# A two-block network on one core: the last projection tiles reordered, and the attention's first maxima and some convolution taps moved across a stage boundary

## What is computed

```python
# first block, chunks of 64 tokens, 4 heads
q, k, v, g_lr, r = split(h @ w_in)                     # 16 columns of g_lr
log_a = log_sigmoid(g_lr @ w_alpha + b_alpha) / 16     # then S_t = diag(a_t) S_{t-1} + k_t^T v_t
o = rmsnorm(q_t S_t per head) * silu(r);  x = rmsnorm(x + gate * (o @ w_out))
# second block
u = rms_norm(x) * (1 + scale) + shift;  p = u @ w_in
q, k = rope_2d(rms_norm(p_q)), rope_2d(rms_norm(p_k))  # 8 query heads, 2 key heads of 64
attn = softmax(q @ [k_ctx, k]^T / 8) @ [v_ctx, v] * silu(p_za)
y = depthwise_conv31(p_a * sigmoid(p_g)) + conv_b      # 512 channels, "124 taps" of 128 channels
conv = (silu(layer_norm(y)) @ w_pw + b_pw) * silu(p_zc)
out = x + gate * ([attn, conv] @ w_out)
```

## Time and profile before

| what | us |
|---|---|
| median of 3 executions (2685.8 to 2707.22) | 2698.7 |
| the profiled execution, its own time | 2696.7 |
| its span in the trace | 2694.9 |
| GLA, of the span | 65.2 to 1053.8 |
| projections, to the end of the last tile | 1063.8 to 1596.1 |
| from there to the attention's first score | 1596.1 to 1646.7 |
| attention's 32 steps | 1646.7 to 2431.7 |
| output | 2431.7 to 2694.9 |

### The profile page before, as it was taken

How to read it: one execution, slowest core, us unless ns; L and a number is a source line. 1 busy time by engine, 2 the same in 40 slices (tenths; PEclk the granted TensorE clock), 3 DMA queues, 4 the chain that set the end, 5 groups by cost and what they waited for, 6 DMA issues and landing times. The chain is left out here.

```text
span 2694.9 us, 34569 instructions
## 1 busy us (share of the span) xinstructions
PE 2495.9 (93%) x11297; PEld 1715.9 (64%) x11297; DVE 1716.4 (64%) x2698; ACT 1011.4 (38%) x1766; POOL 765.3 (28%) x353
## 2 busy tenths in 40 slices
PE   4898899999999998999999966999999999988998
PEld 1576677777777776777777753545544555546776
DVE  3236564654546351888997985777777777775664
ACT  4144453434344430322222124544454444542222
POOL 0233311101111110112202024666667666640000
PEclk8899999999999999999999986999999999998999
DMA  7964787378567747488767544111112101104334
GB/s 263 348 205 145 264 283 273 135 248 317 190 231 267 263 153 263 173 289 307 233 220 252 200 167 103 28 29 29 29 53 59 26 25 29 29 24 162 129 133 155
DMA packets 225098, 453.40 MB, mean 168 GB/s; under 512 B 23941, under 2 KB 82555, under 8 KB 224724
## 3 DMA queue, kind: packets, MB, share of 16 engines
q1 hardware_dynamic: 193928, 351.01, 38.6%
q10 hardware_dynamic: 31052, 100.87, 10.8%
HBM read 328.82 MB, written 109.35 MB: 163 GB/s over the span
## 5 line engine op out<-in xcount | busy, mean ns | idle before, releaser
L2098 DVE TENSOR_REDUCE att_mx<-att_bank_m 128x1 f32<-128x512 f32 (+1 forms) x640 | 365.3, 630 | 126.5 <-PE att_bank_m L1907 126.5
L2047 ACT ACTIVATE att_p_f<-att_bank_s 128x512 f32<-128x512 f32 x576 | 316.9, 597 | 304.4 <-PE att_bank_s L1948 293.5
L557 PE MATMUL gla_bank_g<-mid_a_hi,mid_w_hi 128*128 128x512 f32 x1024 | 417.2, 407 | 13.4 <-DVE mid_a_lo L1075 10.4
L557 PE MATMUL gla_bank_g<-mid_a_lo,mid_w_hi 128*128 128x512 f32 x1024 | 403.2, 394 | 0.0
L557 PE MATMUL gla_bank_g<-mid_a_hi,mid_w_lo 128*128 128x512 f32 x1024 | 403.2, 394 | 0.0
L1888 POOL TENSOR_TENSOR att_den<-att_den,att_p_f 128x1024 f32<-128x1024 f32 x160 | 379.6, 2373 | 59.6 <-ACT att_p_f L2047 48.7
L1611 DVE SCALAR_TENSOR_TENSOR proj_conv_acc<-proj_conv_in,proj_conv_w,proj_conv_acc 128x512 f32<-128x512 f32 (+1 forms) x480 | 362.0, 822 | 0.0
L1922 PE MATMUL att_bank_o<-att_p_f,att_v 128*64 128x512 f32 x1152 | 269.1, 602 | 0.0
L557 PEld LDWEIGHTS gla_bank_g<-mid_a_hi,mid_w_hi 128*128 128x128 f32 x1024 | 195.3, 191 | 77.6 <-issue 19.0
L557 PEld LDWEIGHTS gla_bank_g<-mid_a_hi,mid_w_lo 128*128 128x128 f32 x1024 | 194.7, 190 | 42.4
L557 PEld LDWEIGHTS gla_bank_g<-mid_a_lo,mid_w_hi 128*128 128x128 f32 x1024 | 195.4, 191 | 40.6 <-issue 2.7
(11 more groups left out here) (400 smaller groups left out, 4505.5 us busy)
## 6 DMA issues: line engine op xcount, KB each, us to landing
mid_w_hi<-scratch_w_hi SPq DMA_DIRECT2D x100, 512.0 KB, 4.5
mid_w_lo<-scratch_w_lo SPq DMA_DIRECT2D x100, 512.0 KB, 6.0
mid_w_hi<-scratch_w_hi ACTq DMA_DIRECT2D x84, 512.0 KB, 3.8
mid_w_lo<-scratch_w_lo ACTq DMA_DIRECT2D x84, 512.0 KB, 5.1
scratch_w_hi<-mid_w_hi SPq DMA_DIRECT2D x54, 512.0 KB, 6.2
scratch_w_lo<-mid_w_lo SPq DMA_DIRECT2D x54, 512.0 KB, 7.0
mod_wslab<-in_ada_w SPq DMA_DIRECT2D x6, 2048.0 KB, 17.9
first_w_raw<-in_gla_w_in SPq DMA_DIRECT2D x24, 512.0 KB, 6.5
```

The source lines that it names most:

```text
L557: last = pe.matmul(banks[s % 2][:], w[:, k, :], a[:, k, :], start=(k == 0 and n == 0), stop=(k == KT - 1 and n == 2))
L2047: act.activation(p_f[:, kt, :], S[kt % SBANKS][:], ACT.Exp, scale=float(HD) ** -0.5).then_inc(p_done, 1)
L2098: dve.reduce_max(mx[:, qt, n:n + 1], M[p % MBANKS][:, 0:min(TB, KEYS - TB * n)], AX_X).then_inc(mx_read, 1)
```

## The change

1. The two phases become one. The attention's functions are called inside the projections' program and get their semaphores and PSUM banks (S is BQ, BS, G0; M is BN, BX, BY, BV; the output bank is G1). No barrier stands between the two.
2. In the last block the tiles go in the order 0 to 3, 8 to 13 (q, k, v), 4 to 7, 14 to 21, and the chain of q and k runs 4 turns earlier (`chain_turn`). In every block k's head goes ahead of q's four. SP loads the keys and v of the first three blocks and the context at turn 2 of the last block, and its last 512 keys, q of the first two steps and the last v at turn 16 (7 DMAs, in front of the swap of the fifth head). ACT rounds them at turns 6 and 16.
3. The first step's 20 pieces stand on PE between the last gate tiles: 4 behind each of tiles 17 to 21. DVE takes the maxima of each 4 at the end of the following turn (18 to 21), behind that turn's gate and taps, and the last 4 after turn 21.
4. The last block's table has 86 of the 124 taps. The other 38 go to steps 0 to 6, 5 or 6 a step: 2 at kt 7, 2 at kt 10, the rest behind the column at kt 14.
5. The two multiplications and the addition of the rope are all on DVE (before, POOL had two of the three): 40 more instructions of 128x512 on DVE in the stage, 40 fewer on POOL.
6. In step 0, ACT rounds group 1's keys at kt 8 and sets its row of ones at kt 12; POOL makes their rest (5.05 us before). The first group's steps 1 to 7 are written out instead of looped.
7. GLA: the gate's weights are 32 columns (hi and lo side by side), so 16 matmuls instead of 24 a block; y's hi and lo have tensors of their own, so the next block's input can be rounded while the last w_out tiles run; the gating of six chunks of y takes their first 3/4 early and the last 128 tokens in 2 instructions over three chunks; ACT rounds 7 chunks of y ahead of the tanh of the last r tile; the sum of squares is made one tile earlier (between tiles 4 and 5 of w_out) and the split of the next input within tiles 5 and 6. The first u loads of the projections are issued by SP in the last block's turn 24 instead of after its last tile.
8. Output: other places in memory only.

```diff
     OWN = [[7] * 7 + [6] * 3 + [5] * 2 + [4, 3, 3, 4, 4, 5]] * 2 + [[7] + [6] * 8 + [7] + [6] * 2 + [5] * 2 + [4] * 4] + [
-        [8, 8, 8, 7, 8, 7, 8, 7, 8, 7] + [7, 7, 6, 6, 6, 6, 5, 5]]
+        [7] * 8 + [6] + [0] + [4, 4, 4, 3, 2, 2, 2, 3]]
+    HEADS = (4, 0, 1, 2, 3)
+    EARLY_TILES = 4
+    ORDER = [list(range(NW))] * (NB - 1) + [[0, 1, 2, 3] + list(range(8, 14)) + [4, 5, 6, 7] + list(range(14, NW))]
+    def chain_turn(b, j):
+        return j + EARLY_TILES if b == NB - 1 else j
...
+    SINGLE = 8
+    TAP_STEPS = 7
...
+                        if b == NB - 1 and j == 2:
...
+                            load_made()
+                        if b == NB - 1 and jq == 20:
+                            sp.wait_ge(v_stored, UP + 16 * NB)
+                            sp.wait_ge(q_stored, UP + 16 * (5 * (NB - 1) + 1))
+                            load_last()
...
+        def first_maxima(first):
+            if first == 0:
+                pe.wait_ge(k_hi_done, UP + 2)
+            for p in range(first, first + 4):
+                piece(0, 0, 0, p)
...
+                        if b == NB - 1:
+                            if j == 16:
+                                split_first_q()
+                            if j >= 18:
+                                first_maxima(4 * (j - 18))
+                first_maxima(16)
+                first_column()
+                rest()
...
+        def taps_of_step(dve, i, part):
+            if isinstance(i, int) and i < TAP_STEPS:
+                m0, m1 = last_tap[i], last_tap[i + 1]
+                third = -(-(m1 - m0) // 3)
+                keep["last_taps"](dve, min(m0 + third * part, m1), min(m0 + third * (part + 1), m1))
```

More of the change, by code:

```diff
@@ L551, in gemm @@
                     for k in range(KT):
-                        if k == BETWEEN_AT and between is not None:
+                        if k == between_at and between is not None:
                             between()
@@ new lines, in attention, with col, tiles_in @@
+    w_raw = [k_raw[0][:, D * n:D * (n + 1)] for n in range(2)]
+    y = k_raw[0][:, 0:NC * TB].rearrange("p (k n) -> p k n", k=NC)
+    acc, rs = (k_raw[1][:, TB * n:TB * (n + 1)] for n in (2, 3))
+    squares = (q_raw[0], q_raw[1])
+    tanhs = (den[0][:, 0, :], den[0][:, 1, :], q_raw[0][:], q_raw[1][:])
+    BM, BV = M[1], M[2]
+    def col(name, j):
+        at = VROWS[name][0] + j
+        return cols[:, at:at + 1]
+    def tiles_in(i):
+        return W_AT[i] if isinstance(i, int) and i in W_AT else ()
@@ new lines, in at_step, with need, pair, steps @@
+    def at_step(i, n):
+        return isinstance(i, int) and i == n
+    def need(eng, semaphore, n):
+        if isinstance(n, int) and n <= 0:
+            return
+        eng.wait_ge(semaphore, UP + n)
+    def pair(j):
+        return p_f[:, 2 * j:2 * j + 2, :]
+    def steps(eng, body):
+        last = GROUP_STEPS - 1
+        for g in range(NKV):
+            base = g * GROUP_STEPS
+            body(base, 0, g, g - 1 if g else None, g)
+            single = 2 if g else SINGLE
+            for n in range(1, single):
+                body(base + n, n % 2, g, g, g)
+            with eng.Fori(single // 2, GROUP_STEPS // 2 - 1) as it:
+                for s in range(2):
+                    body(it * 2 + (base + s), s, g, g, g)
+            body(base + last - 1, 0, g, g, g)
+            body(base + last, 1, g, g, g + 1 if g + 1 < NKV else None)
@@ new lines, in gpsimd, with rest_of_k, body @@
+    def gpsimd(pool):
+        def rest_of_k(n):
+            g, keys = K_PARTS[n]
+            pool.wait_ge(k_hi_done, UP + n + 1)
+            pool.tensor_tensor(k_b[g][0:HD, keys], k_raw[g][0:HD, keys], k_a[g][0:HD, keys].bitcast(F32), ALU.subtract).then_inc(k_lo_done, 1)
+        pool.wait_ge(k_hi_done, UP + 1)
+        pool.memset(mz[:], 0.0).then_inc(cleared, 1)
+        rest_of_k(0)
+        rest_of_k(1)
+        def body(i, s, g, before, after):
+            need(pool, den_sum, i - 1)
+            for j in range(1, POOL_ADDS + 1):
+                if j == 5 and at_step(i, 0):
+                    rest_of_k(2)
+                pool.wait_ge(p_done, UP + i * NKT + 2 * j + 2)
+                if j > 1:
+                    pool.wait_ge(den_pool, UP + i * POOL_ADDS + j - 1)
+                pool.tensor_tensor(den[s][:], pair(0) if j == 1 else den[s][:], pair(j), ALU.add).then_inc(den_pool, 1)
+            for n in tiles_in(i):
+                if n >= 2:
+                    pool.wait_ge(w_hi_done, UP + n + 1)
+                    pool.tensor_tensor(wo_lo[:, n - 2, :], w_raw[n % 2], wo_hi[:, n - 2, :].bitcast(F32), ALU.subtract).then_inc(w_lo_done, 1)
+        steps(pool, body)
@@ new lines, in body, with first_maxima, rest @@
+                            rest_wp(n)
+                    add_den(i, s, NPR - 2)
+                if kt == 17 and at_step(i, STEPS - 2):
+                    centre_y()
+        def first_maxima(first):
+            for p in range(first, first + 4):
+                reduce(0, p)
+        def rest():
+            steps(dve, body)
+            add_den(STEPS - 1, 1, NPR - 1)
+            fold_den(STEPS - 1, 1)
+            swish_y(0)
+            swish_y(1)
+            add_o(STEPS - 1)
+            swish_y(2)
+            invert(STEPS - 1)
+            swish_y(3)
+            finish(STEPS - 1)
+            for k in range(NC):
+                rest_y(k)
```

1252 lines of the change are left out of this document (652 added, 600 removed).

## The result

Four executions of the changed kernel took 2719.87 to 2736.26 us, median 2729.16; four of the kernel before 2685.8 to 2707.22, median 2699.74. The ratio is 1.0124 (95% interval 1.0094 to 1.0154): slower by 29 us, or 1.2%. The forecast was 2716 in a range of 2664 to 2745. The time lies in the range, but the largest chance, 0.47, stood on "within 1%", and slower by more had 0.31.

The account below looks back on a forecast made before the run. PE, with work in 93% of the span, was taken to bound the kernel, its clock second. 2696.7 - 18 - 3.5 + 0 - 6 + 45 = 2714.2, with 2.0 for the median 2716 us; range 2664 to 2745.

Parts of the forecast that it names:

- GLA's gain: GLA, part 7: fewer matmuls, shorter waits and less half clock, against a longer wait L658; -18 us, bounds -5 to -40.
- the step from a profiled execution to the median: Whole kernel: the median lies 2.0 us above the profiled execution, as before, making 2714.2 into 2716.
- The attention: Attention, parts 4 and 6: taps delay maxima and column, so PE waits and its clock falls; +45 us, bounds +5 to +60.
- One tap per addition: Attention: DVE gets in one tap per POOL addition, so two taps count as 4.2 us, not 1.4.
- The boundary: Between projections and attention, parts 1 to 3: overlap against waits behind tiles and half clock; -6 us, bounds -14 to +15.
- C: Rival: PE stays at half clock through the last gate tiles (10 us each) and most of steps 1 to 6; 2746 us, chance 0.16.
- The gap to the projections: GLA to projections: loads issued 7 tiles earlier shorten PE's 10.0 us wait; -3.5 us, between 0 and -4.5.
- the rope: Projections, blocks 0 to 2: ten more DVE operations a block, offset by fewer collisions with POOL; 0, between -3 and +6 us.
- the output: Output stage: nothing of its work changes; 0, within 2 us.
- the waits for y: GLA: of PE's 10.4 us of waits for the rests of y, 4 go.
- L658's wait: GLA block ends: PE's 5.7 us wait on DVE's chain stays and grows by 2 at each of three boundaries, 6 us.
- a second tap right behind the first: Attention: by the port lock it could keep the ports and cost 0.7 us, making the sum some 30 us less.

Follow-up runs that it names:

- e13: The changed kernel measured once more, with no edit, beside the other runs on one chip; median 2724.94 us, ratio 1.0107 to the kernel before.
- e1: The changed kernel without the 38 taps of the attention's steps 0 to 6; median 2680.29 us, ratio 0.9947 to the kernel before.
- e2: The changed kernel with all taps, POOL's additions in steps 0 to 6 left out but for 8 columns; median 2682.56 us, ratio 0.9946.
- e4: The changed kernel with DVE's four maxima of turns 18 to 21 at the head of the turn; median 2699.06 us, ratio 1.0018.
- e11: e7 with ACT's tanh of the last r tile in GLA behind 3 roundings of y instead of 7; 2680.58 us, ratio 0.9941.
- e12: e7 with e11's earlier tanh, the first q loaded early and block 0's w_out weights rounded ahead of the next input; 2677.55 us, ratio 0.9932.
- e15: e7 with first q early, 3 taps in turn 17, 27 in 12 attention steps, block 0's w_out weights rounded ahead of the next input; 2667.27 us.
- e7: e4 with 16 taps back in turns 14 to 21, 22 in 11 attention steps, early-key pieces first, last keys rounded in turn 18; 2666.5 us.
- e8: e4 with all 124 taps in the last block's turns of the projections, none in the attention; 2667.37 us, ratio 0.9889.
- e3: The changed kernel with all of a step's 5 or 6 taps behind the column at kt 14; median 2719.45 us, ratio 1.0098.
- e9: e7 with the first step's q loaded at turn 2 instead of behind the store of the last k; 2669.98 us, ratio 0.9898.

## Why the forecast was right and wrong

**What failed.** The forecast was 13 us too low (2716 against 2729.2). Two terms of its sum were mis-sized. The first is GLA's gain, taken as 18: it was 16.0 in the first trace and 10.6 by the median of twelve (below). The second is the step from a profiled execution to the median, taken as 2.0 from the kernel before: in the changed kernel it was 9.3, and 6.3 in e13, and both times the profiled execution was the shortest of its four. The profiled executions were short by 5.7 (2.0 in GLA, 2.7 in the attention, 1.3 in the output), the step to the median by 7.3. In which stage the longer executions lose these us stays open, since only profiled executions have a trace. And a forecast of +17 whose terms of gain were the less certain ones should have put more than 0.31 on "slower by over 1%".

**The attention** (+45; measured +47.7 and +38.3 in two executions). Shown: e1 and e2 put all of it on taps that meet POOL's additions. "One tap per addition" gave 4.2 us for a pair, measured 4.32 at kt 7 and 5.72 at kt 10. The split of a step's loss was wrong: the forecast had 5.7 us of waits and 1 of clock, measured were 2.6 and 3.5 as a mean of steps 0 to 6. PE doesn't have to stand 3.7 us at one place for its clock to fall; in the step from 1741.26 it stood 0.95 and 0.70 at the maxima of kt 10 and the clock was at the half level for 6.8 us soon after. But the two sizes are not independent errors that cancelled by luck. Where the clock stayed full up to the transposes PE waited there 3.36 (step 5) and 3.37 us (step 2 of e13), as the forecast's 3.7 had it; in the other steps 1 to 6 of the two traces it was at the half level for 6.8 to 10.2 us before them and PE waited 0 to 0.36; and all twelve took 28.0 to 30.5 us. So most of the half-clock time stands where the wait would have been, and in seven of the twelve steps the late column alone set when the transposes began. In the other five PE came 1.7 to 3.2 us behind the column, against 1.0 before: there the slow clock added something of its own.

**The boundary** (-6; from the end of tile 17 to the first score -8.3, and the stage ahead of it took 1.8 more, which makes the table's -6.6). 61.7 us of terms and 7 of clock against 66.5 measured: waits of 6.8 (5 forecast), 5.1, 4.3, 4.3 and 5.2 (5.8 and more forecast), and half clock for 35 of the 66.5 us. e4 shows that the order of the maxima made the four waits. C (tiles of 10 us throughout) was wrong: a tile's 24 matmuls took 6.9 to 7.3, since the clock fell in each wait and rose again within each tile.

**The gap to the projections** (-3.5; -3.3), **the rope** (0; in the 1.8 just named) and **the output** (0; +1.3, and 1.1 to 1.9 in all fifteen traces of the changed kernel and its variants, cause not looked for) need no more.

**GLA** (-18; -16.0 and -10.4). Twelve of the fifteen traces have GLA's code unchanged (all but e11, e12 and e15). It ended at 1037.8 to 1050.2, with a median of 1043.1, against 1053.7 in the one trace of before. The first trace of the changed kernel is the shortest of the twelve, and that its gain came near 18 was luck. From the first weight tile the twelve took 965.4 to 976.9 us, before 980.6, and they differ mostly by the clock: it was at the half level for 20.5 us in the first trace, 34.1 in e13 and 44.4 in e2 (the longest), and for 44.4 before. The two with 44.4 us at half clock, as before, gained 4 and 7 us. The start moved too: PE's first matmul of GLA came 1.1 to 4.1 us later in all fifteen than in the one of before; why stays open. Three steps of the term were wrong. Of the waits for y, 4 of 10.4 were to go, and 1.4 went. L658's wait was to grow by 6, and fell from 5.7 to 0.8: DVE's chain, begun one tile earlier, ends in time. And a wait that the forecast doesn't have came in: in block 0 ACT rounds w_out's weights as it goes, and the next input's rounding, moved into the same turns, waits for DVE in front of them (10.0 us in all for weights, 2.8 before; that this order makes the one of 3.8 is shown by e15).

The Trainium skill ("SBUF — State Buffer", section "Who interferes with whom") states that a DVE instruction with two SBUF inputs contends with a GpSimd instruction that reads SBUF. e2 agrees: a tap took 0.76 us with the additions cut to 8 columns and 1.9 beside whole ones. That a second tap right behind the first might keep the ports and cost 0.7 was the forecast's own reading of the lock, and it did not come true: pairs took 4.32 and 5.72.

The versions e7 (2666.5), e15 (2667.3) and e8 (2667.4) beat both kernels, the kernel before by 1.1%. e8 needs the fewest changes to the changed kernel: the maxima at the head of the turn and all taps in the projections.

## What to carry to other kernels

Idle time of DVE beside a GpSimd engine that adds all the time is not room: for operations such as these taps (two inputs from SBUF), count there one per GpSimd operation, not its own duration. When the last results of one stage are interleaved with the next, put what another engine waits for ahead of what waits for the other engine; the order within one turn was worth 26 us here, more than the whole overlap gave. And look at what stands behind a run of moved operations on its own engine, not only behind the wait that it fills: that is where e3 and e9 lost. Last, one trace of a stage is one draw: here GLA differed by 12 us between executions of the same code, as much as most terms of the forecast.
